# Two transformer blocks on one core: state inputs laid out by place, and a new order of convolutions and block inputs in the mixer

## The reference

```python
u = rmsnorm(h, norm_mix) @ w_in
u_pool, u_ssm = u[..., :512], u[..., 512:]
y_pool = pool_mixer(u_pool, w_pool, pool_scale)
y_ssm = ssm_mixer(u_ssm, lam_re, lam_im, log_dt, b_re, b_im, c_re, c_im, d_skip, w_glu, b_glu)
h = h + concatenate([y_pool, y_ssm]) @ w_out
h = h + (silu(n @ w_gate) * (n @ w_up)) @ w_down        # n = rmsnorm(h, norm_ffn)
return rmsnorm(h, norm_final)
```

```python
s[t] = a * s[t-1] + bbar @ u[t]
y[t] = real(c @ s[t]) + d_skip * u[t]
y = gelu(y);  y = y * sigmoid(y @ w_glu + b_glu)
```

## Time and profile before

| | |
|---|---|
| time before, median of 3 runs | 2301.35 us (2301.0 to 2301.77) |
| the profiled execution | 2299.97 us |
| its span on the core | 2298.2 us |
| PE busy | 2271.8 us, 99% |
| weight loads busy | 1894.6 us, 82% |
| DVE, ACT, POOL busy | 965.7, 971.3, 1144.7 us |
| mean granted clock of PE | 0.997 |

### The profile page before, as it was taken

The page is one execution under the profiler, slowest core; times in us unless marked ns, Lnnn a source line. Parts: engine busy times, 40 slices in busy tenths (PEclk is TensorE's granted clock), DMA queues, the critical chain, the costliest instruction groups (busy, mean ns, idle before and its releaser), DMA issues.

```text
span 2298.2 us, 32267 instructions
## 1 busy us (share of the span) xinstructions
PE 2271.8 (99%) x11672; PEld 1894.6 (82%) x11672; DVE 965.7 (42%) x1589; ACT 971.3 (42%) x1344; POOL 1144.7 (50%) x702
## 2 busy tenths in 40 slices
PE   8999999999999999999999999999999999999998
PEld 7888888888888887888888888888888778888886
DVE  6355442344543204554453343344376774222201
ACT  5444442254555325444353343555522535444321
POOL 3433325578984455333244465444455666444452
PEclk9999999999999999999999999999999999999999
DMA  5222223322223332222222223332333113323321
GB/s 210 81 73 80 90 81 101 101 85 95 93 89 110 128 101 79 75 80 89 73 89 92 97 78 102 100 100 91 101 110 110 56 38 110 100 93 99 101 92 55
DMA packets 61283, 214.17 MB, mean 93 GB/s; under 512 B 7200, under 2 KB 7456, under 8 KB 61216
## 3 DMA queue, kind: packets, MB, share of 16 engines
q1 hardware_dynamic: 58480, 205.63, 27.5%
q10 hardware_dynamic: 2736, 7.63, 1.0%
HBM read 211.13 MB, written 2.10 MB: 93 GB/s over the span
## 4 chain that ended last, share of the span: by engine, by line
PE 98%; DVE 1%; DMA 0%; ACT 0%; issue 0%; SPq 0%; DVEq 0%; ACTq 0%
PE psum L833 87%; PE psum L866 4%; PE psum L870 2%; PE psum L1222 1%; PE psum L968 1%; PE psum L955 1%; PE psum L932 1%; PE psum L1237 0%; PE psum L1248 0%; DMA z<-in_x 0%; PE psum L1007 0%; PE psum L1044 0%; PE psum L861 0%; PE psum L862 0%; DVE out_t L2164 0%; PE psum L942 0%
## 5 line engine op out<-in xcount | busy, mean ns | idle before, releaser
L467 POOL TENSOR_TENSOR w_lo<-stage,w_hi 128x1024 fp32r<-128x1024 f32 x378 | 922.4, 2448 | 1057.0 <-ACT w_hi L1370 1041.7
L833 PE MATMUL psum<-xh,w_hi 128*128 128x512 f32 x1712 | 668.3, 390 | 0.7 <-DVE scaled L2386 0.7
L833 PE MATMUL psum<-xh,w_lo 128*128 128x512 f32 x1712 | 666.2, 389 | 0.0
L833 PE MATMUL psum<-xl,w_hi 128*128 128x512 f32 x1712 | 666.2, 389 | 0.0
L1370 ACT ACTIVATE w_hi<-stage 128x1024 fp32r<-128x1024 f32 x377 | 396.6, 1053 | 375.0 <-PE psum L833 373.8
L833 PEld LDWEIGHTS psum<-xh,w_hi 128*128 128x128 f32 x1712 | 321.4, 188 | 68.1 <-DVE na_q_lo L1868 1.7
L833 PEld LDWEIGHTS psum<-xh,w_lo 128*128 128x128 f32 x1712 | 321.4, 188 | 67.4
L833 PEld LDWEIGHTS psum<-xl,w_hi 128*128 128x128 f32 x1712 | 321.5, 188 | 65.7
L833 PE MATMUL psum<-g_hi,w_hi 128*128 128x512 f32 x528 | 206.2, 391 | 0.0
L833 PE MATMUL psum<-g_hi,w_lo 128*128 128x512 f32 x528 | 205.4, 389 | 0.0
L833 PE MATMUL psum<-g_lo,w_hi 128*128 128x512 f32 x528 | 205.4, 389 | 0.0
(11 more groups left out here) (401 smaller groups left out, 3351.1 us busy)
## 6 DMA issues: line engine op xcount, KB each, us to landing
stage<-in_w SPq DMA_DIRECT2D x380, 512.0 KB, 3.4
bias_raw<-in_bias ACTq DMA_DIRECT2D x8, 384.0 KB, 3.0
z<-in_x SPq DMA_DIRECT2D x3, 512.0 KB, 7.9
out_x<-out_t SPq DMA_DIRECT2D x3, 512.0 KB, 2.7
p_raw<-in_p ACTq DMA_DIRECT2D x2, 512.0 KB, 3.4
masks_raw<-in_masks SPq DMA_DIRECT2D x1, 576.0 KB, 11.3
masks_raw<-in_masks ACTq DMA_DIRECT2D x1, 576.0 KB, 4.5
z<-in_x SPq DMA_DIRECT2D x2, 256.0 KB, 4.3
```

What stands on the lines that cost most here:

```text
L467: pool.tensor_tensor(w_lo[s][:, :, :], stage[s][:, :, :], w_hi[s][:, :, :].bitcast(F32), ALU.subtract).then_inc(lo_done, 1)
L833: mm = pe.matmul(dst, lhs[i], rhs[j], start=start and n == 0, stop=stop and n == 2)
```

## The change

The inputs of groups 1 to 3 are copied by ACT, so that the 128 tokens of one place lie side by side. The copies go to `u_all[:, q, :]`, q = 1 to 3, which hold nothing yet: DVE writes the pooling inputs there later, after the block inputs of the same q have been read. `block_inputs(q)` reads the copy for q = 1 to 3 and the strided original for q = 0, and waits for `u_placed` in place of the bank's own semaphore. On PE, block inputs 1 stand ahead of convolution 0, and convolution 1 moves forward to just behind block inputs 2. On ACT, `ahead(2)`, which rounds unit 5 (the sixth), moves from ahead of the last four copies of `w_b2` and of `k_conv` to behind them, and the three new copies stand between `scan_table(0)` and `scan_table(1)`.

```diff
+        u_placed = sem("ssm_input_by_place")
...
                 def block_inputs(q):
 
-                    pe.wait_ge(*after_result(MIX, MIN_R0 + q))
                     if q:
+                        pe.wait_ge(u_placed, q)
                         pe.wait_ge(v_read, q)
+                    else:
+                        pe.wait_ge(*after_result(MIX, MIN_R0))
+
+                    def at_place(r0, j):
+                        if q:
+                            return u_all[r0:r0 + 2 * SCH, q, j * NB:(j + 1) * NB]
+                        return by_place(u_all[r0:r0 + 2 * SCH, SP_T, :])[:, :, j]
+
...
-                                               by_place(u_all[r0:r0 + 2 * SCH, 4 + q, :])[:, :, j],
+                                               at_place(r0, j),
...
                 in_unit(4, take_bank(MIX, MIN_R0 + 4))
+                block_inputs(1)
                 convolve(0)
-                block_inputs(1)
                 in_unit(5, take_bank(MIX, MIN_R0 + 5))
                 block_inputs(2)
+                convolve(1)
                 in_unit(6, take_bank(MIX, MIN_R0 + 6))
                 block_inputs(3)
-                convolve(1)
                 from_state(0)
...
                 ahead(1)
-                ahead(2)
                 for j in range(BT - 3, -1, -1):
                     b_apart(j)
...
+                def by_place(q):
+                    act.wait_ge(*after(MIN_R0 + q))
+                    act.activation(u_all[:, q, :].rearrange("p (j b) -> p j b", j=BT),
+                                   u_all[:, SP_T + q, :].rearrange("p (b j) -> p j b", j=BT), ACT.Copy).then_inc(u_placed, 1)
+
+                ahead(2)
                 ahead(3)
...
                 scan_table(0)
+                by_place(1)
+                by_place(2)
+                by_place(3)
                 scan_table(1)
```

## The result

The changed kernel takes **2303.3 us** in the median of its runs (2302.03 to 2305.56), the kernel before 2300.93 (2298.53 to 2302.49) beside it on the same chip. The ratio is 1.0013, with a 95% interval of 1.0007 to 1.0019: 3.0 us slower by the ratio, between 1.6 and 4.4 (2.4 by the medians). That lies inside the 4.6 us called no change, and inside the range. The profiled execution took 2304.35 with a span of 2302.6, that of before 2299.97 with 2298.2; some of these 4.4 us is chance, as will be seen.

The account below looks back on a forecast made before the run. PE was taken as the bound (98% of the span), with VectorE and GpSimd close behind. Savings of 0.93 and 6.0 us become waits on VectorE; +1.2 us remain, taking the median 2301.35 to 2302.5, range 2298.2 to 2305.8.

Parts of the forecast that it names:

- rivals 1 and 2: State part: VectorE escapes its stalls, net -1 to -3 us, chance 0.33; or stalls once more, PE +3.6 us, chance 0.17.
- (a): Ahead of the state part: the sixth unit rounded later lets PE's block inputs 0 start 0.93 us earlier, at 1808.65.
- (b): PE's block inputs: contiguous sets 1 to 3 take 1.8 us each, which is 6.0 us less PE work.
- rival 5: PE's block inputs: weight loads pace the sets, not the stride; no long wait, VectorE and GpSimd +0.8, 2302.1; chance 0.12.
- (c): ScalarE's three copies take 0.53 us each; a GpSimd low part then stalls VectorE 1.7 us; VectorE's chain shifts +0.8 us.
- the later stall of 2.2 us: VectorE's operation of line 2271, stretched to 2.88 us from 0.68 under a GpSimd low part, was assumed to stay.
- rival 2: State part: two VectorE stalls against GpSimd instead of one; VectorE +3.1, with the clock PE +3.6 us, 2305.0; chance 0.17.
- (d): PE idles 4.5 us for VectorE ahead of convolution 2, then meets late GpSimd at unit 13: net +0.8 us.
- (e): Behind PE's 4.5 us wait the clock falls to 1.2 GHz, costing up to 3.1 us; the resulting +1.2 us decides.

Follow-up runs that it names:

- the gated kernel: The changed kernel with three GpSimd waits, holding the low parts of units 7, 8 and 9 until VectorE finishes a state tile each; 2297.53 us, ratio 0.9988.
- runs with one and two gates: The changed kernel with a GpSimd wait before unit 9's low part alone (2301.37 us), or before those of units 8 and 9 (2300.2 us).

## Why the prediction was right, and where it wasn't

**The time and the sign** were right: 2302.5 was forecast against a median of 2301.35, that is +1.2 us, and +2.4 by the medians (+3.0 by the ratio) was measured. The range, 7.6 us wide, held rivals 1 and 2 as well, so that the time lies in it says little of the mechanism. The way there was only half right.

- **(a) Block inputs 0 earlier by 0.93: in effect.** The issue idle of 1.02 us went, but the start moved only from 1809.58 to 1809.19. In this execution of the changed kernel the clock showed 0.66 between 1784 and 1788 us, far ahead of the changed part; in the kernel before, in the gated kernel and with the copies left unread it showed 1.00 there, and in the latter two block inputs started at 1808.14 and 1808.20. This is part of the 4.4 us between the spans that the medians don't confirm.
- **(b) Sets of 1.8 us: nearly.** They take 2.07 by PE's timeline, and the strided set 0 still 3.89. The weight loads didn't pace them: rival 5 falls.
- **(c) Copies of 0.53 us: wrong.** They take 1.06, the upper end given (1.0). Unit 7's low part therefore ran from 1815.83 instead of 1814.3, and met line 2273's operation in place of line 2271's, for 2.2 us instead of 1.7.
- **(c) "With the later stall of 2.2 us kept as it is": this is the step that failed.** That stall was kept, in another operation, but unit 9's low part, which the sum left losing to VectorE for good as in the kernel before, lost only at first and then stalled the scans for 2.1 us. VectorE's chain is three stalls long instead of two: -0.9 + 6.5 - 2.2 = +3.4 us on that chain instead of +0.8. That is the VectorE part of rival 2 (+3.1), given 0.17. The runs with one and two gates show each stall as a step of its own.
- **(d) A wait of 4.5 us ahead of convolution 2: right** (4.28), with two smaller ones that the timetable didn't have (1.33 and 2.02), since VectorE was later than assumed. That GpSimd bounds unit 13 was right, and it is the key to the whole: PE's 5.5 us of spared work come to nothing while GpSimd is late. (A reading under it was off: when VectorE's last result is there, at 1855.36, PE has the whole pair of state outputs still to do, 1855.60 to 1859.20, of which only half needs that result.)
- **(e) The clock falls: right; that it decides: hardly.** The convolutions took 2.8 us more because of it (7.88 against 5.09). Its bound of 3.1 us should have been 3.4, half of the 6.8 us at half speed. Filling the wait took the 2.8 us away; the median didn't fall, and in the traces unit 13 came 0.9 us sooner. The sum let the clock add 0.4 us to GpSimd's lateness, and the runs can't tell 0.4 from 0 or from 0.9.

So the forecast missed 2.6 us on VectorE's chain: a third stall of 2.1 us, and 0.5 us on the first. Its nearness to the measured time is in part luck. Against the medians the corrected chain, +3.4, is somewhat high; the difference of 0.4 to 1.0 us is within the interval and wasn't taken apart further.

## What to carry to other kernels

Work taken off the busiest engine is worth only what the next chain behind it leaves; follow that chain (here VectorE, then GpSimd's pooling) to the instruction where the busiest engine meets it again, and measure edits by distances along it. Where two engines lock each other out, moving either by a microsecond can make or remove whole stalls: don't carry a stall of the old trace, or its absence, into the new timetable, but place the movable work by a wait into the stretch where the other engine needs no lock. A change that loses and a wait that does nothing by itself can win together.

## What the runs showed of the hardware

- **A stride of four fp32 elements nearly doubles the time on ScalarE and on PE:** 1.06 us for a strided copy of 128x512 (0.53 for a contiguous square of that size), and 3.89 against 2.07 us for a set of 64 matmuls of 128 columns. The Trainium skill (Advanced Engine Details and Errata, SBUF Cachelines) says that lines in SBUF hold 16 bytes and that reading a different one at every access is penalised; a step of 16 bytes does that. The factor, 1.9 to 2 on these two engines, is this case's.
- **64 weight loads of 32 rows can be through in 1.9 us** when the matmuls between them are short, where they spanned 3.50 in the strided set; the matmuls had paced the loads.
- **Who wins a collision turns on tenths of a microsecond, counted from the start of VectorE's operation.** GpSimd's instruction was served next when it came 0.41 us behind (unit 8 in the kernel before) and 0.28 us behind (unit 7 in the changed kernel, 1815.83 against 1815.55). It had to stand when it came 0.09 us behind (unit 9 before, 5.27 us), 0.12 us behind (unit 9 in the changed kernel, 1830.06 against 1829.94) and 0.17 us behind (pooling started early, 1849.52 against 1849.35). Where it stood, it stood over several instructions of VectorE's, up to 3.4 us. The Trainium skill (SBUF — State Buffer, SBUF: two separate sides) says that the first to start has the ports for the whole instruction; the sizes agree with that, but the rule doesn't say who is next when one engine has its next instruction ready at once. Five cases are no rule, and the reason stays open.
- **Scans take part in it too:** pairs of 2.33 us were stretched to 4.48 and 4.44.
- **The same wait isn't always followed by a fall of the clock.** Ahead of the state part, where nothing was changed, PE waits 1.9 us in the window from 1780 to 1784 us in each of the 13 profiled executions. The granted clock was 1.00 from 1784 to 1788 in five of them, and 0.57 to 0.70 in eight. Two profiles of one kernel can differ by it ahead of the part that one looks at.
